# Attention in three passes of high and low parts, with the gating of VectorE and the values of TensorE in another order

## What is computed

```python
def block_attention(q, k, v):          # q (1,512,8,128), k and v (1,768,2,128)
    scale = hd ** -0.5                 # in blocks of 128 queries
    s = jnp.einsum('bqkgd,bskd->bkgqs', qi, k) * scale
    p = jax.nn.softmax(s, axis=-1)
    return jnp.einsum('bkgqs,bskd->bqkgd', p, v)
b_lat = block_attention(q_lat, keys, vals) * jax.nn.silu(bz)
x_new = x + gate * ((g_a * (a_lat @ w_proj_a) + g_b * (b_lat @ w_proj_b)) @ w_out)
```

## Time and profile before

| what | us |
|---|---|
| time, median of 3 runs | 1899.73 (1896.98 to 1901.27) |
| the profiled execution, its own time | 1899.6 |
| its span in the profile | 1897.4 |
| PE busy, share of the span | 1807.1, 95% |
| DVE busy | 911.5, 48% |
| ACT busy | 660.9, 35% |
| POOL busy | 276.7, 15% |
| attention, first scores to the last values' end | 1408.5 to 1632.5 |
| granted clock, mean | 0.987 |
| PE's share of the chain that ended last | 82% |

### The profile page before, as it was taken

One profiled execution on the slowest core, in us unless ns is written; L12 is line 12 of the kernel. 1 busy time (PEld: TensorE's weight loads), 2 busy tenths in 40 slices (PEclk: granted clock), 3 DMA queues, 4 the chain that ended last, 5 costly groups with the idle time before them and its releaser, 6 DMA issues.

```text
span 1897.4 us, 25274 instructions
## 1 busy us (share of the span) xinstructions
PE 1807.1 (95%) x10174; PEld 1445.0 (76%) x10174; DVE 911.5 (48%) x1595; ACT 660.9 (35%) x1211; POOL 276.7 (15%) x421
## 2 busy tenths in 40 slices
PE   5799999999999998999999999999999889999999
PEld 2367888888787877788888888877876566688887
DVE  1244443556424565555565553764365544453333
...
GB/s 302 238 321 127 56 56 56 63 71 90 72 56 177 171 172 138 163 186 151 144 124 135 119 103 219 215 209 212 152 121 85 89 78 84 246 187 100 122 122 100
DMA packets 198684, 267.12 MB, mean 141 GB/s; under 512 B 37072, under 2 KB 135625, under 8 KB 197161
## 3 DMA queue, kind: packets, MB, share of 16 engines
...
## 4 chain that ended last, share of the span: by engine, by line
PE 82%; DVE 6%; DMA 4%; ACT 4%; issue 3%; POOL 0%; SPq 0%; ACTq 0%; DVEq 0%; POOLq 0%
PE psum L1611 23%; PE psum L1613 21%; PE psum L1612 21%; PE psum L1916 2%; PE psum L1759 1%; PE psum L1710 1%; PE psum L1708 1%; DVE L_upper L1185 1%; DVE w_lo L1091 1%; PE psum L1936 1%; DMA w_raw_mod<-w_mod_dram 1%; PE psum L1903 1%; PE psum L1604 1%; PE psum L1716 1%; ACT w_hi L759 1%
## 5 line engine op out<-in xcount | busy, mean ns | idle before, releaser
L1091 DVE TENSOR_TENSOR w_lo<-w_raw,w_hi 128x1024 fp32r<-128x1024 f32 x232 | 289.1, 1248 | 642.4 <-ACT w_hi L759 642.0
L759 ACT ACTIVATE w_hi<-w_raw 128x1024 fp32r<-128x1024 f32 x232 | 245.5, 1058 | 863.4 <-PE psum L1613 774.4
L1611 PE MATMUL psum<-h_hi,w_hi 128*128 128x512 f32 x1152 | 473.1, 411 | 22.5 <-DVE w_lo L1091 20.3
L1613 PE MATMUL psum<-h_hi,w_lo 128*128 128x512 f32 x1152 | 453.4, 394 | 0.0
L1612 PE MATMUL psum<-h_lo,w_hi 128*128 128x512 f32 x1152 | 453.0, 393 | 0.0
L1611 PEld LDWEIGHTS psum<-h_hi,w_hi 128*128 128x128 f32 x1152 | 218.4, 190 | 83.9 <-DVE w_lo L1091 21.6
L1613 PEld LDWEIGHTS psum<-h_hi,w_lo 128*128 128x128 f32 x1152 | 218.0, 189 | 49.3
L1612 PEld LDWEIGHTS psum<-h_lo,w_hi 128*128 128x128 f32 x1152 | 219.0, 190 | 36.3
L1161 DVE SCALAR_TENSOR_TENSOR conv_acc<-conv_in,convw,conv_acc 128x772 f32<-128x772 f32 x96 | 98.2, 1023 | 3.4
L1611 PE MATMUL psum<-w_hi,m_hi 128*128 128x512 f32 x256 | 99.6, 389 | 0.0
L1612 PE MATMUL psum<-w_lo,m_hi 128*128 128x512 f32 x256 | 99.6, 389 | 0.0
...
## 6 DMA issues: line engine op xcount, KB each, us to landing
...
```

The source lines that it names most:

```text
L759: act.activation(part(whi[i % 2], p), part(place, p), ACT.Copy).then_inc(S("w_hi"), 1)
L1091: dve.tensor_tensor(part(wlo[i % 2], p), part(raw_of(n)[0], p), part(whi[i % 2], p).bitcast(f32), ALU.subtract).then_inc(S("w_lo"), 1)
L1611: pe.matmul(out_ap, lh, rh, start=first, stop=False, skip_group_check=shared)
L1613: return pe.matmul(out_ap, ll, rh, start=False, stop=last, skip_group_check=shared)
```

## The change

Scores and values go through `three`. For this the queries, keys, values and transposed probabilities get a high part, which ScalarE writes where it wrote plain copies before (`q_hi`, `k_hi`, `pt_hi`, and a new one over the values, `v_hl`), and a low part, which VectorE subtracts (`q_lo_part` for 8 heads, the keys of two key heads, one instruction of 6 x 256 for the values, and `pt_lo_part` in each of the 32 steps: two instructions of 4 x 128 and 2 x 128 for heads 0 to 5, one of 6 x 128 for heads 6 and 7). TensorE's waits for scores, values and transposes move from ScalarE's copies to VectorE's low parts. VectorE's order changes: `b_parts` is split, and `pa_gated` now stands between `b_gated` and `b_lo_part`. On TensorE `values` moves behind the half piece and `q_transposes` ahead of it. On ScalarE `q_columns` moves ahead of the copy of the probabilities. The semaphores of several zeroed buffers are merged into one, `zeroed`; order and waits of those instructions stay as they were. The diff, cut to its core:

```diff
     pa_gate = [at(f"pa_gates{i}", [P, 512], A_H + 53248 + 2048 * i) for i in range(2)]
     pa_out = [at(f"pa_stage{i}", [P, 512], A_H + 57344 + 2048 * i) for i in range(2)]
     sqj = at("square_out", [P, P], A_T + 12288)
-    qhT = at("att_qT", [P, HEADS, SEQ], A_H)
-    khT = at("att_kT", [P, KV, TOK], A_H + 16384)
-    PTt = at("probsT", [P, NT, SEQ], A_H + 34816)
+    q_hi = at("att_q_hi", [P, HEADS, SEQ], A_H, f32r)
+    q_lo = at("att_q_lo", [P, HEADS, SEQ], G_V + 16384, f32r)
+    k_hi = at("att_k_hi", [P, KV, TOK], A_H + 16384, f32r)
+    k_lo = [at(f"att_k_lo{kv}", [P, TOK], (A_H + 30720, A_T + 8192)[kv], f32r) for kv in range(KV)]
+    v_hl = at("att_v", [P, NT, 512], A_C + 16384, f32r)
+    pt_hi = at("probsT_hi", [P, NT, SEQ], A_H + 34816, f32r)
+    pt_lo_a = at("probsT_lo_a", [P, 4, 1024], A_C, f32r)
+    pt_lo_b = at("probsT_lo_b", [P, 2, SEQ], G_V + 12288, f32r)
+    pt_lo_c = at("probsT_lo_c", [P, NT, SEQ], A_H, f32r)
     atmp = [at(f"a_tmp{i}", [P, 512], A_C + 2048 * i) for i in range(2)]
     probs = [at(f"probs{i}", [P, TOK], A_H + 47104 + 3072 * i) for i in range(2)]
     cs = at("cos_sin", [P, LT, 128], G_V)
...
             if g["kind"] == "pa":
                 if g["m"] == 0:
                     eng.wait_ge(S("a_lo"), HEADS)
-                    eng.wait_ge(S("kt_evac"), KV)
+                    eng.wait_ge(S("att_lo"), 6)
                 else:
                     eng.wait_ge(S("pa_mul"), g["m"])
             if g["kind"] == "merge":
...
 
             def q_columns(h, b):
                 act.wait_ge(S("qt_ready"), h + 1)
-                act.activation(qhT[:, h, :], bank(b), ACT.Copy).then_inc(S("qt_evac"), 1)
+                act.activation(q_hi[:, h, :], bank(b), ACT.Copy).then_inc(S("qt_evac"), 1)
 
             for kv in range(KV):
                 q_columns(2 * kv, 2 * kv)
                 q_columns(2 * kv + 1, 2 * kv + 1)
                 act.wait_ge(S("kt_ready"), kv + 1)
-                act.activation(khT[:, kv, :], PS[:, (4 + 2 * kv) * 512:(4 + 2 * kv) * 512 + TOK], ACT.Copy).then_inc(
+                act.activation(k_hi[:, kv, :], PS[:, (4 + 2 * kv) * 512:(4 + 2 * kv) * 512 + TOK], ACT.Copy).then_inc(
                     S("kt_evac"), 1)
 
             def att_exp(i):
...
                 h, qt = divmod(i, 4)
                 if qt == 0 and h >= 1:
                     act.wait_ge(S("pv_done"), h)
+                if qt == 2 and 3 <= h < 7:
+                    q_columns(h + 1, 6)
                 act.wait_ge(S("pt_ready"), i + 1)
-                act.activation(PTt[:, :, qt * P:(qt + 1) * P],
+                act.activation(pt_hi[:, :, qt * P:(qt + 1) * P],
                                PS[:, 2048:2048 + TOK].rearrange("p (t n) -> p t n", t=NT), ACT.Copy).then_inc(
                     S("pt_evac"), 1)
                 if i < 4:
                     q_squares(1, i)
                 if i == 4:
                     qk_std(3, 16, 32)
-                if qt == 2 and 3 <= h < 7:
-                    q_columns(h + 1, 6)
+                if i == 1:
+                    act.activation(v_hl[:, :, 0:256], kvr[:, :, 256:512], ACT.Copy).then_inc(S("kt_evac"), 1)
                 if qt == 1 and h >= 1:
                     act.wait_ge(S("b_tmp"), h)
                     act.activation(b_hi[:, h - 1, :], btmp[:], ACT.Copy).then_inc(S("b_hi"), 1)
...
                 dve.tensor_scalar(nmax[:, i:i + 1], nmax[:, i:i + 1], -float(HD ** -0.5), None, ALU.mult).then_inc(
                     S("negmax"), 1)
 
-            def b_parts(h):
+            def b_gated(h):
                 dve.wait_ge(S("pv_done"), h + 1)
                 k = HEADS + h
                 dve.wait_ge(S(f"z_in{k % 2}"), 16 * (k // 2 + 1))
                 dve.tensor_tensor(btmp[:], bank(6), zst[k % 2][:], ALU.mult).then_inc(S("b_tmp"), 1)
+
+            def b_lo_part(h):
                 dve.wait_ge(S("b_hi"), h + 1)
                 dve.tensor_tensor(b_lo[:, h, :], btmp[:], b_hi[:, h, :].bitcast(f32), ALU.subtract).then_inc(S("b_lo"), 1)
 
...
                     dve.wait_ge(S(f"pa_spill{m % 2}"), 16 * (m // 2))
                 dve.tensor_tensor(pa_out[m % 2][:], bank(7), pa_gate[m % 2][:], ALU.mult).then_inc(S("pa_mul"), 1)
 
+            def q_lo_part(h, b):
+                dve.wait_ge(S("qt_evac"), h + 1)
+                dve.tensor_tensor(q_lo[:, h, :], bank(b), q_hi[:, h, :].bitcast(f32), ALU.subtract).then_inc(S("att_lo"), 1)
+
+            def pt_lo_part(i):
+                h, qt = divmod(i, 4)
+                own = slice(qt * P, qt * P + P)
+                dve.wait_ge(S("pt_evac"), i + 1)
+                src = PS[:, 2048:2048 + TOK].rearrange("p (t n) -> p t n", t=NT)
+                if h >= 6:
+                    dve.tensor_tensor(pt_lo_c[:, :, own], src, pt_hi[:, :, own].bitcast(f32), ALU.subtract).then_inc(S("pt_lo"), 1)
+                    return
+                dve.tensor_tensor(pt_lo_a[:, :, own], src[:, 0:4], pt_hi[:, 0:4, own].bitcast(f32), ALU.subtract)
+                dve.tensor_tensor(pt_lo_b[:, :, own], src[:, 4:6], pt_hi[:, 4:6, own].bitcast(f32), ALU.subtract).then_inc(
+                    S("pt_lo"), 1)
+
+            for kv in range(KV):
+                q_lo_part(2 * kv, 2 * kv)
+                q_lo_part(2 * kv + 1, 2 * kv + 1)
+                if kv:
+                    for i in range(2):
+                        dve.wait_ge(S(f"gate_spill{i}"), 16 * len(GATES))
+                dve.wait_ge(S("kt_evac"), kv + 1)
+                dve.tensor_tensor(k_lo[kv][:], PS[:, (4 + 2 * kv) * 512:(4 + 2 * kv) * 512 + TOK],
+                                  k_hi[:, kv, :].bitcast(f32), ALU.subtract).then_inc(S("att_lo"), 1)
+
             att_max(0)
             for i in range(32):
                 dve.wait_ge(S("exp_done"), i + 1)
                 ln(dve.reciprocal(rsum[:, i:i + 1], rsum[:, i:i + 1]))
                 dve.tensor_scalar(probs[i % 2][:], probs[i % 2][:], rsum[:, i:i + 1], None, ALU.mult).then_inc(
                     S("p_norm"), 1)
+                if i:
+                    pt_lo_part(i - 1)
                 if i < 31:
                     att_max(i + 1)
+                if i % 4 == 2 and 3 <= i // 4 < 7:
+                    q_lo_part(i // 4 + 1, 6)
                 if i % 4 == 1 and i >= 5:
-                    b_parts(i // 4 - 1)
+                    b_gated(i // 4 - 1)
                 if i % 2:
                     pa_gated(i // 2)
                 else:
                     lo_part(N_PA0 + i // 2 + 1)
-
+                if i % 4 == 1 and i >= 5:
+                    b_lo_part(i // 4 - 1)
+
+                if i == 2:
+                    dve.wait_ge(S("kt_evac"), 3)
+                    dve.tensor_tensor(v_hl[:, :, 256:512], kvr[:, :, 256:512], v_hl[:, :, 0:256].bitcast(f32),
+                                      ALU.subtract).then_inc(S("att_lo"), 1)
                 if i == 4:
                     qk_var(44, 16, 32)
                 if i == 5:
                     qk_rstd(3, 16, 32)
                 if i in (6, 7, 10, 11):
                     q_tile(1, (6, 7, 10, 11).index(i))
+            pt_lo_part(31)
             lo_part(N_MERGE0 + 1)
-            b_parts(HEADS - 1)
+            b_gated(HEADS - 1)
+            b_lo_part(HEADS - 1)
             for n in range(N_MERGE0, NP):
                 if n > N_MERGE0:
                     lo_part(n + 1)
...
                 h, qt = divmod(i, 4)
                 if i < 2:
 
-                    pe.wait_ge(S("qt_evac"), 2 * i + 2)
-                    pe.wait_ge(S("kt_evac"), i + 1)
+                    pe.wait_ge(S("att_lo"), 3 + 2 * i)
                 else:
                     pe.wait_ge(S("exp_done"), i - 1)
                 if h >= 4 and qt == 0:
-                    pe.wait_ge(S("qt_evac"), h + 1)
+                    pe.wait_ge(S("att_lo"), h + 4)
                 b = 2 * (i % 2)
-                q = qhT[:, h, qt * P:(qt + 1) * P]
+                q = tuple(part[:, h, qt * P:(qt + 1) * P] for part in (q_hi, q_lo))
                 kv = h // (HEADS // KV)
-                pe.matmul(bank(b), q, khT[:, kv, 0:512], start=True, stop=True)
-                pe.matmul(bank(b + 1, 256), q, khT[:, kv, 512:TOK], start=True, stop=True).then_inc(S("sc_ready"), 1)
+                three(bank(b), q, (k_hi[:, kv, 0:512], k_lo[kv][:, 0:512]), True, True)
+                three(bank(b + 1, 256), q, (k_hi[:, kv, 512:TOK], k_lo[kv][:, 512:TOK]), True, True).then_inc(S("sc_ready"), 1)
 
             def values(h):
 
-                pe.wait_ge(S("pt_evac"), 4 * h + 4)
+                pe.wait_ge(S("pt_lo"), 4 * h + 4)
                 if h >= 1:
                     pe.wait_ge(S("b_tmp"), h)
+                if h == 0:
+                    pe.wait_ge(S("att_lo"), 7)
                 if 3 <= h < 7:
 
-                    pe.wait_ge(S("qt_evac"), h + 2)
+                    pe.wait_ge(S("att_lo"), h + 5)
                 kv = h // (HEADS // KV)
                 for t in range(NT):
```

(19 more changed lines are left out.)

24 lines of the change are left out of this document (12 added, 12 removed).

## The result

The changed kernel takes 1901.26 us (median of 20 runs, 1897.03 to 1908.02), the kernel before 1895.74 (20 runs, 1888.09 to 1901.27): ratio 1.0036 [1.0025, 1.0048], 0.36% slower, 6.8 us with 4.7 to 9.1 (the two medians themselves lie 5.5 apart). Forecast was 3.3 us faster. The time lies inside the range, the direction was wrong.

What follows compares the result with a forecast made beforehand. PE was taken to bound the attention stage, VectorE's queue steps 4 to 11. Terms 0.2 + 2.95 + 2.5 - 8.4 - 0.6 = -3.3 took 1899.6 to 1896.3 us, range 1889 to 1904.

Steps and rivals of the forecast that it cites:

- heads 3 to 6: Later attention heads: 25.77 us each against 27.87, 8.4 us won in four, with the queries' wait growing to 3.35.
- steps 0 to 3: First attention head: fourth transposes start at 18.3 instead of 14.1, values end at 26.95 against 24.01, 2.95 us lost.
- the walk: Link-by-link timing of the attention stage's queues, giving 1896.3 us; chance 0.6 that it holds within 2.5 us either way.
- What follows depends on that end as before: Behind the attention stage: the rest follows the end of the last values unchanged, so no term was added.
- Heads 1 and 2: Steps 4 to 11: VectorE's queue with the query tiles bounds; 29.9 and 29.5 us, together 59.4 against 56.89, 2.5 lost.
- the last head: Steps 28 to the end: values end at 25.25 against 25.85, 0.6 us won.
- PE's prices: PE's work in scores and values: scores 1.05 us instead of 1.29, values 4.13 instead of 5.15, 15.7 less in all.
- VectorE's prices: New low-part subtractions on VectorE: `pt_lo_part` 0.95 us until VectorE goes on, some 40 us more in all.
- rival 2: `pt_lo_part` is dear, 14 times on the path: up to 1904.8 us; chance 0.12 together with rival 4.
- rival 3: Instructions run without overlap or links are a tenth longer: 2 us more, 1898.5, no change; chance 0.11.
- Rival 4: The waits for `pa_gated` stay, 7 x 1.45: 1906 us; chance 0.12 together with rival 2.
- Rival 1: PE alone bounds heads 3 to 6, 22.4 us each: 1883 us, or 1891.7 for half; chance 0.17 whole or half.

Runs made afterwards that it cites:

- fill_q_wait: The changed kernel with 12 idle passes ahead of TensorE's wait for the queries' low part, four times: 1895.48 us, ratio 0.9992 to the kernel before.
- before_longer_wait: The kernel before with six small ScalarE copies ahead of the copy of the next head's queries, four times: 1909.65 us, ratio 1.0063.
- fill_all_waits: fill_q_wait with 13 more idle passes ahead of the last transposes of head 0 and 19 for heads 1 and 2: 1898.05 us, ratio 1.0007.
- split_first: The changed kernel with queries, values' parts and the next piece's rounding moved earlier, and query tiles moved to GpSimd: 1858.01 us, ratio 0.9804.

## Why the prediction was wrong

**The step that failed** is in the part on heads 3 to 6: "This wait was 1.48 and becomes 3.35: here half of the gain is lost". The length of the wait was right (3.2), its price was not. I priced it as idle time only and let the scores and the piece behind it run at the pace of the earlier trace rows, where PE had waited 1.5 us at most. They ran at half clock. The same holds in steps 0 to 3: the walk put the fourth transposes at 18.3 instead of 14.1, which came out (18.31), with a long wait of PE, and let the scores, the half piece and the values behind it run at full clock. Where PE's work is on the path, the slow spells cost 1.5 + 2.7 + 1.65 + 1.67 + 1.54 = 9.1 us. With these the sum of -3.3 becomes +5.8, inside the measured 4.7 to 9.1. "What follows depends on that end as before" did not hold either: the spell behind the stage cost 1.6, which makes +7.4, inside as well. For four of the five spells in the stage and for the mechanism the cause is shown from both sides: fill_q_wait takes the spell away and leaves the chain, before_longer_wait makes the spell without the change. For head 0 it is what fill_all_waits shows behind the fourth transposes (8.57 us against 10.17). The spell behind the stage was not tested by filling its wait.

**Luck.** That the time lies inside the range owes something to the base: I summed from the profiled execution's 1899.6, which is 3.9 us above the median of the 20 runs. From 1895.74 the same sum gives 1892.4.

**What held.**
- The chains. Heads 1 and 2 came within 0.1 us, the last head exactly, and heads 3 to 6 at full clock in fill_q_wait within 0.06. In head 5 the four steps took 4.45, 4.91, 9.50 and 8.58; the walk had 4.45, 4.9, 7.8 and 8.6: the whole miss is in the third.
- PE's prices. Nine value passes took 1548.85 - 1546.80 = 2.05, 0.228 each, so eighteen cost the 4.1 predicted. Transposes and scores together took 1550.55 - 1548.85 = 1.70, as 0.65 and 1.05 make.
- VectorE's prices, none of which had a row: `pt_lo_part` 0.68 and 0.41, begun 0.60 apart, 0.94 until VectorE goes on (predicted 0.95). So rival 2 falls, and rival 3 with it, since no link was longer.
- Rival 4: the wait for `pa_gated` is gone. What the change says it does, it does.

**Heads 1 and 2** were right although PE waited 4.8 us there ahead of the last transposes and their clock was 0.89 and 0.94. There VectorE's queue bounds the steps behind the wait, and the slow passes lay beside it; fill_all_waits shows the reverse.

**A side figure** was off: a quarter of PE's old work on scores and values, 32 x 1.29 + 8 x 5.15 = 82.5 us, is 20.6, not the 19 given for it. The sum did not use it.

**Rival 1** was wrong for the changed kernel (27.4, not 22.4) and right as a description of where PE's bound lies: split_first reaches it. I gave it for the wrong kernel: what was missing were four moves of other work (queries, values' parts, tiles, rounding) that stands ahead of what PE waits for.

**The rivals as a set** held no case in which PE's work itself gets dearer. The slower side was given to a price on VectorE. The traces of before could not show it, since PE there never waited long enough in this stage; but the walk did make waits of 3.35 us and more, which had no row. The price of such a wait should have had bounds from both sides: its upper bound is not its length but its length and the work behind it at half clock.
